# Borders of mixer and post norms joined to their neighbours, attention over two heads at a time

## The reference: what is computed

```python
# first block
h = rmsnorm(x, norm_mix_pre); proj = h @ w_in            # pool, glu, gate_a, gate_b parts
branch_a = pool_mixer(u_pool, ...) ; branch_b = conformer_conv(u_glu, ...)   # conv of 31 taps, layernorm, silu
merged = sigmoid(g_a) * branch_a + sigmoid(g_b) * branch_b
x = x + rmsnorm(merged @ w_o, norm_mix_post)
h = rmsnorm(x, norm_mlp_pre)
x = x + rmsnorm(square(relu(h @ w_up)) @ w_down, norm_mlp_post)
# second block
h = x + deltanet_mixer(rmsnorm_2(x, a_norm), ...)        # 8 heads
h = h + conv_ffn(...)
kv = rmsnorm_2(h, kv_norm) @ kv_w + kv_b                 # 4 key/value heads of 64
h = h + swa_sink_attention(rmsnorm_2(h, b_norm), k, v, w_q, b_q, sinks, w_o, b_o)
h = h + conv_ffn(...)
return rmsnorm_2(h, final_norm)
# attention: 16 heads of 64, blocks of 128 queries that see their own and the previous 128 keys
s = q @ k.T + bias; m = max(max(s), sink); p = exp(s - m)
o = (p @ v) / (sum(p) + exp(sink - m))
```

## Time and profile before

| | |
|---|---|
| three runs | 2055.31, 2057.66, 2059.57 us; median 2057.66 |
| profiled execution | 2061.48 us, span 2059.7 us |
| PE busy | 1969.4 us, 96% of the span |
| DVE, ACT, POOL busy | 1262.3, 765.3, 291.8 us |
| mean granted clock of PE | 0.978 of full speed |
| HBM | 82 GB/s over the span |

### The profile page before, as it was taken

The page is one execution under the profiler, slowest core; times in us unless marked ns, Lnnn a source line. Parts: engine busy times, 40 slices in busy tenths (PEclk is TensorE's granted clock), DMA queues, the critical chain, the costliest instruction groups (busy, mean ns, idle before and its releaser), DMA issues.

```text
span 2059.7 us, 27282 instructions
## 1 busy us (share of the span) xinstructions
PE 1969.4 (96%) x9454; PEld 1631.0 (79%) x9454; DVE 1262.3 (61%) x1826; ACT 765.3 (37%) x1350; POOL 291.8 (14%) x215
## 2 busy tenths in 40 slices
PE   6999889999998899999999999999989999999997
PEld 5878677888887688888887788888778787888886
DVE  5886545333334777777755755737668657657374
ACT  4233344232233433444434433424535434324242
POOL 2433123011112200000012100101100011001011
PEclk9999889999999899999999999999999999999998
DMA  4323231333323011111113232232301132323322
GB/s 172 101 76 90 81 123 62 102 102 92 101 91 105 21 47 51 56 56 46 46 42 94 81 104 90 93 101 92 123 31 42 41 102 82 103 92 92 103 92 82
DMA packets 46922, 170.10 MB, mean 83 GB/s; under 512 B 5344, under 2 KB 5504, under 8 KB 46720
## 3 DMA queue, kind: packets, MB, share of 16 engines
q1 hardware_dynamic: 45648, 165.12, 25.4%
q10 hardware_dynamic: 1200, 3.95, 0.6%
HBM read 166.94 MB, written 2.11 MB: 82 GB/s over the span
## 4 chain that ended last, share of the span: by engine, by line
PE 76%; DVE 7%; issue 2%; ACT 2%; POOL 0%; DVEq 0%; POOLq 0%; ACTq 0%
PE ps L246 16%; PE ps L247 16%; PE ps L248 16%; PE ps L258 6%; PE ps L260 6%; PE ps L259 6%; PE ps L594 2%; PE ps L610 2%; PE ps L1132 1%; PE ps L1157 1%; PE ps L598 1%; DVE scr L1074 1%; PE ps L1143 1%; DVE A_lo L362 1%; DVE X L1932 1%
## 5 line engine op out<-in xcount | busy, mean ns | idle before, releaser
L226 DVE TENSOR_TENSOR w_lo<-w_raw,w_hi 128x1024 fp32r<-128x1024 f32 x293 | 394.9, 1350 | 184.3 <-ACT w_hi L221 184.2
L221 ACT ACTIVATE w_hi<-w_raw 128x1024 fp32r<-128x1024 f32 x304 | 316.9, 1048 | 235.3 <-PE ps L248 169.5
L246 PE MATMUL ps<-A_hi,w_hi 128*128 128x512 f32 x964 | 377.1, 391 | 10.6 <-DVE scr L917 5.0
L247 PE MATMUL ps<-A_lo,w_hi 128*128 128x512 f32 x964 | 376.6, 391 | 0.0
L248 PE MATMUL ps<-A_hi,w_lo 128*128 128x512 f32 x964 | 376.3, 390 | 0.0
L246 PE MATMUL ps<-B_hi,w_hi 128*128 128x512 f32 x732 | 286.8, 392 | 5.4 <-issue 2.4
L247 PE MATMUL ps<-B_lo,w_hi 128*128 128x512 f32 x732 | 285.7, 390 | 0.0
L248 PE MATMUL ps<-B_hi,w_lo 128*128 128x512 f32 x732 | 285.6, 390 | 0.0
L258 PE MATMUL ps<-A_hi,w_hi 128*128 128x512 f32 x460 | 202.0, 439 | 27.5 <-DVE w_lo L226 13.0
L246 PEld LDWEIGHTS ps<-A_hi,w_hi 128*128 128x128 f32 x964 | 181.6, 188 | 50.6 <-issue 12.8
L248 PEld LDWEIGHTS ps<-A_hi,w_lo 128*128 128x128 f32 x964 | 181.9, 189 | 38.1
(11 more groups left out here) (253 smaller groups left out, 2701.0 us busy)
## 6 DMA issues: line engine op xcount, KB each, us to landing
w_raw<-d_ws SPq DMA_DIRECT2D x304, 512.0 KB, 3.5
X<-d_xT SPq DMA_DIRECT2D x4, 512.0 KB, 7.2
X<-d_xT ACTq DMA_DIRECT2D x1, 2048.0 KB, 7.8
d_out<-X SPq DMA_DIRECT2D x4, 512.0 KB, 2.7
scr<-gc_rows ACTq DMA_DIRECT2D x7, 256.0 KB, 3.1
cst<-d_cst SPq DMA_DIRECT2D x1, 800.0 KB, 11.7
par<-d_par SPq DMA_DIRECT2D x1, 344.5 KB, 3.3
scr<-d_pw SPq DMA_DIRECT2D x1, 256.0 KB, 12.4
```

What stands on the lines that cost most here:

```text
L221: nc.scalar.activation(w_hi[:, c], raw[:, c], ACT.Copy).then_inc(S(f"w_hi{s}"), 1)
L226: nc.vector.tensor_tensor(w_lo[:, c], raw[:, c], w_hi[:, c].bitcast(F32), ALU.subtract)\
L246: pe.matmul(ps[bank][:], w_hi[:, c], hi, start=k == 0, stop=False)
L247: pe.matmul(ps[bank][:], w_hi[:, c], lo, start=False, stop=False)
```

## The change

- `spread` uses transposes in place of matmuls with the identity.
- In the first glu round both engines make the splits of the next round's first two units before they evacuate.
- The pool mixer has four buffers UP in place of two, and DVE no longer waits for POOL there.
- At the layer norm `ln_hi` and `ln_lo` of a tile stand one tile later, and the split of branch unit 3 stands before the loop.
- At post0, post1 and fin `sums_early` stands before the last block of the last unit. At post0 the last square is taken from PSUM. Splits on the chain are moved behind it (post0: one, post1: both). In `add_normed` the low part of the previous tile stands before the addition to X.
- Attention: SC and PT have two buffers each, so four with the two heads; scores, transposes and values of both heads of a tile are issued together, scores in two halves of two query blocks, with banks 2 and 3 now belonging to the heads and not to the halves. `part` is cut into 2, 3 and 3 blocks. The query split on ACT and DVE moves by one unit.

```diff
-        UP = [X[...], VATH[:, 0:UPW]]
+        UP = [X[...], VATH[:, 0:UPW], SQ[:, 0:UPW], Y[...]]
...
-                last = pe.matmul(ps[bank][:, c * P:(c + 1) * P], src[:, c:c + 1].broadcast_to([P, P]), ident,
-                                 start=True, stop=True)
+                last = pe.transpose(ps[bank][:, c * P:(c + 1) * P], src[:, c:c + 1].broadcast_to([P, P]), ident)
...
+        def last_unit(pe, r, pair, tag, bank):
+            unit_wait(pe, r, SLOTS - 1)
+            part_blocks(pe, 1, SLOTS - 1, pair, 0, KT - 1)
+            sums_early(pe, tag, KT, bank)
+            part_blocks(pe, 1, SLOTS - 1, pair, KT - 1, KT).then_inc(S(f"unit_done{SLOTS - 1}"), 1)
...
-        def scores_pe(pe, j):
+        def scores_pe(pe, t, n):
+            if n == 0:
+                pe.wait_ge(S("q_t"), count("q_t", t + 1))
+            if t or n:
+                pe.wait_ge(S("s_sc"), count("s_sc", 4 * t + 2 * n))
+            for b in (2 * n, 2 * n + 1):
...
+                for e in range(2):
+                    out = ps[2 + e][:, (b % 2) * 256 + 256 - size:(b % 2) * 256 + 256]
+                    last = pe.matmul(out, half_rows(QT[t % 2], e)[:, b * P:(b + 1) * P],
+                                     half_rows(KA[t % 2], e)[:, lo:lo + size], start=True, stop=True)
...
-            for j in range(2 * KT):
-                t, e = j // 2, j % 2
-                if j < 2 * KT - 1:
-                    scores_pe(pe, j + 1)
-                transpose_pe(pe, j)
-                if e == 0:
-                    part(t + 1, KT // 2, KT)
-                else:
-                    part(t + 2, 0, KT // 2)
-                values_pe(pe, j)
+            scores_pe(pe, 0, 0)
+            part(1, 2, 5)
+            scores_pe(pe, 0, 1)
+            part(1, 5, KT)
+            for t in range(KT):
+                if t < KT - 1:
+                    scores_pe(pe, t + 1, 0)
+                part(t + 2, 0, 2)
+                if t < KT - 1:
+                    scores_pe(pe, t + 1, 1)
+                transpose_pe(pe, t, 0)
+                part(t + 2, 2, 5)
+                transpose_pe(pe, t, 1)
+                part(t + 2, 5, KT)
+                values_pe(pe, t)
...
+            for e in range(2):
+                exps(0, e)
+            ahead(act, split_hi, rnd(U_Q, 0), 0)
+            for t in range(KT):
+                if t < KT - 1:
+                    ahead(act, split_hi, rnd(U_Q, (t + 1) // SLOTS), (t + 1) % SLOTS)
...
+            scored(0, 0)
+            scored(0, 1)
+            maxima(0, 0)
+            maxima(0, 1)
+            ahead(dve, split_lo, rnd(U_Q, 0), 0)
+            q_tile(1)
+            normalise(0, 0)
+            normalise(0, 1)
+            for t in range(KT):
+                more = t < KT - 1
+                if more:
+                    scored(t + 1, 0)
+                    ahead(dve, split_lo, rnd(U_Q, (t + 1) // SLOTS), (t + 1) % SLOTS)
+                    scored(t + 1, 1)
+                    maxima(t + 1, 0)
+                    maxima(t + 1, 1)
+                if t:
+                    output_lo(t - 1)
+                if more:
+                    normalise(t + 1, 0)
+                    if t + 2 < KT:
+                        q_tile(t + 2)
+                    normalise(t + 1, 1)
...
             def glu_round(i, first):
+                if first:
+                    for k in range(2, SLOTS):
+                        ahead(act, split_hi, rnd(U_GLU, i), k)
+                    norm_row(act, "n0")
                 for k in range(SLOTS):
-                    if first and k == 0:
-                        norm_row(act, "n0")
-                    if not first or k > 1:
+                    if not first:
...
+                    if m == KT - 1:
+                        square(act, "post0", m, ps[k % 2][:], 0.5)
                     nc.scalar.activation(tile(Y, m), ps[k % 2][:], ACT.Copy, scale=0.5).then_inc(S(f"evac{k}"), 1)
...
+                    if m:
+                        norm_lo(dve, next_tag, next_g, pairA, m - 1)
                     dve.wait_ge(S(tag + "_t"), count(tag + "_t", m + 1))
                     v.tensor_tensor(tile(X, m), tile(X, m), t, ALU.add).then_inc(S(xtag), 1)
-                    if m:
-                        norm_lo(dve, next_tag, next_g, pairA, m - 1)
...
             token_mean(dve, "post0", 4, D)
-            ahead(dve, split_lo, rnd(U_MLP, 0), 1)
             dve.wait_ge(S("x_back"), count("x_back", 16))
             add_normed("post0", "x1", "mix_post", 5, "n1", "mlp_pre")
+            ahead(dve, split_lo, rnd(U_MLP, 0), 1)
...
-            for k in range(2):
-                ahead(dve, split_lo, rnd(U_DELTA, 0), k)
             add_normed("post1", "x2", "mlp_post", 5, "na", "a_norm")
+            ahead(dve, split_lo, rnd(U_DELTA, 0), 0)
```

More of the change, by code:

```diff
@@ L927, in residual_pe @@
             for i in range(2):
-                for s in range(0 if i else 2, SLOTS):
+                for s in range(0 if i else 2, SLOTS - (closing and i)):
                     unit(pe, rnd(base, i), s, pair, n)
@@ L996, in wait_mid @@
                     pe.wait_ge(S(t + "_lo"), count(t + "_lo", first + k + 1))
-                residual_pe(pe, down, mid, wait_mid, n)
+                last = end and first + n == 22
+                residual_pe(pe, down, mid, wait_mid, n, closing=last)
+                if last:
+                    unit_wait(pe, rnd(down, 1), SLOTS - 1)
+                    part_blocks(pe, 1, SLOTS - 1, mid, 0, n - 1, n)
+                    sums_early(pe, "fin", KT, 4)
+                    part_blocks(pe, 1, SLOTS - 1, mid, n - 1, n, n).then_inc(S(f"unit_done{SLOTS - 1}"), 1)
         def ffn_act(act, L, base, mid, ntag, next_tag, next_g, next_pair, end=False):
@@ L1611, in _, with mlp_group @@
             for i in range(2):
-                for s in range(0 if i else 2, SLOTS):
+                for s in range(0 if i else 2, SLOTS - i):
                     unit(pe, rnd(U_WO, i), s, pairA)
+            last_unit(pe, rnd(U_WO, 1), pairA, "post0", 4)
             norm_pe(pe, "post0", bank=4)
-            def mlp_group(g, first):
+            def mlp_group(g, first, last=False):
                 if first:
@@ L1627, in mlp_group @@
                 for i in range(2):
-                    for s in range(0 if i else 2, SLOTS):
+                    for s in range(0 if i else 2, SLOTS - (last and i)):
                         unit(pe, rnd(U_MLP, g * 4 + 2 + i), s, pairB)
@@ L1701, in _, with ln_hi @@
                 ahead(act, split_hi, rnd(U_BRANCH, 0), k)
+            def ln_hi(j):
+                act.wait_ge(S("ln_z"), count("ln_z", j + 1))
+                nc.scalar.activation(tile(pairB[0], j), tile(CV, j), ACT.Copy).then_inc(S("ln_hi"), 1)
             for j in range(4):
@@ L1710, in _ @@
                     .then_inc(S("ln_th"), 1)
-                act.wait_ge(S("ln_z"), count("ln_z", j + 1))
-                nc.scalar.activation(tile(pairB[0], j), tile(CV, j), ACT.Copy).then_inc(S("ln_hi"), 1)
+                if j:
+                    ln_hi(j - 1)
+            ln_hi(3)
             for k in range(SLOTS):
@@ L1786, in _ @@
             token_mean(dve, "n0", 2, D)
+            for k in range(2, SLOTS):
+                ahead(dve, split_lo, rnd(U_GLU, 0), k)
             def glu_round(i, first):
```

224 lines of the change are left out of this document (109 added, 115 removed).

## The result

The changed kernel takes 2026.07 us (median of four runs, 2025.56 to 2026.37), the kernel before beside it 2058.61 us; the ratio is 0.9844, 95% interval 0.9829 to 0.986. The profiled execution takes 2025.56 us with a span of 2023.8 us, at a mean granted clock of 0.987 in place of 0.978. One execution of all, of the kernel under "A split beside the power", took 3472.6 us at a granted clock of 0.722 and is left out of its median. The forecast was 2026.0 us. The total is right; the parts are not all.

What follows compares the result with a forecast made beforehand. PE, busy 96% of the span, bounds the kernel through work, waits and half clock. Borders 16.4 plus attention 15.4 make 31.8 us off the 2057.7 us median: 2026 us; own range 2018 to 2034, whole range 2016 to 2046.

Steps and rivals of the forecast that it cites:

- Glu border, 5.2 us: Start of the gate units: PE's 3.6 us wait for w_lo and 1.7 us of half clock go, 5.2 us kept.
- Pool buffers, nothing: Pool mixer: four buffers cost and gain nothing, since the wait for POOL isn't in the ring that holds PE.
- Layer norm, 5.7 us: Layer norm border: PE's wait for gated_pool(3) falls from 6.4 to 2.2 us, half clock gains 1.3 us; 5.7 us in all.
- Post norms: Chains at post0, post1, fin: shorter power and spread, less 0.9 us each for sums_early; gains 2.4, 1.1 and 0.15 us.
- I set it at nothing, with 1 us either way: Other order in add_normed: first low part 0.6 us sooner, last about as much later, so no net gain or loss.
- Borders in all: Everything outside attention: 5.2 + 5.7 + 2.4 + 1.1 + 0.15 + 1.8 = 16.4 us gained.
- I take sharing: Middle of attention: both heads' matmuls share the array, a tile falls from 14.1 to 12.1 us; 17.4 us with the ends.
- DVE ... becomes the floor: Middle of attention: DVE, busy 11.3 us a tile, sets the length once PE shares; 0.8 us of handovers make 12.1.
- the ring of DVE, PE and ACT: Rival, attention tile: its ring becomes the bound, 18.1 us without overlap, slower from 16.1 us on; 2071 us, chance 0.05.
- Attention, start, end and clock: Start loses 6.6 us (8.7 us wait for q_tile(1), 1.6 us for two normalises); end gains 1.9, half clock 2.7.
- the borders weren't given back: Rival: glu border's lead ends in the gate stretch, layer norm's drop keeps its length; 5.2 + 3.4 less, 2035 us, chance 0.12.
- no sharing: Rival, attention: the two heads' matmuls don't share the array, 17.4 us of gain fall out; 2043 us, chance 0.25.

Runs made afterwards that it cites:

- A split beside the power: Changed kernel with the low split of the first delta unit again between mean and add_normed at post1: 2028.57 us (median of three).

## Why the prediction was right, and where it was not

**Glu border, 5.2 us:** right; the run that undoes it gives 5.2 by medians.

**Pool buffers, nothing:** right.

**Layer norm, 5.7 us:** right in size; the run that undoes it gives 5.4, of it 5.1 in the stretch. The wait left is 2.8 us, not 2.2 (its own terms, 6.4 less 3.9, give 2.5), and the drop fell to 3.4 us as chosen. In the table the border shows more (5.7 us with 0.9 lost to `sums_early`), since a second drop of 3.4 us, at 252 us before, is gone too.

**Post norms.** The power at 1.02 us and the spread at half are both shown by undoing them. The copy and the split in front of the mean at post0, 1.3 us together, no run undoes. Post0's chain gave 4.0 us, not 3.3; 0.5 of it is the earlier first low part, which the run with the old order in `add_normed` loses again. `sums_early` costs 0.9 us at each border, as forecast, and at post1 0.7 us more: I counted its matmuls, and not that behind the longer wait the last sums mostly run at half clock.

**`add_normed`, "I set it at nothing, with 1 us either way":** wrong, the step of the borders that failed. I counted the tile's instructions by durations from elsewhere and asked which tile's low part came when. What counts is what runs beside them. The new order puts the addition to X beside POOL's squares, and both borders lose 2.9 us. The first low part does come 0.5 to 0.6 us sooner, so the order costs 4.6 us in all where I had nothing. The price stood in the rows that I used: the power that takes 1.93 us beside a split is the same exclusion with the engines' parts changed over, and I applied it to POOL alone.

**Borders in all:** forecast 16.4. The table without attention's 21.6 us (22.1 less a spread's 0.45) sums to 14.3 us; without the 5.7 us of `add_normed` it would be 20. What came on top of the forecast, 3.6 us, is mostly clock. Three stretches gave 1.35, 0.9 and 0.95 us more than forecast, and in each a drop fell away or became 3.4 us shorter: near 252, 710 and 1717 us of the kernel before. The last two places the change doesn't touch. In all, PE's clock was at half for 92 us before and for 55 now. Since executions of one kernel differ in such drops, part of this is chance.

**Attention, middle.** "I take sharing": right. The two heads' matmuls take 3.8 us together in place of 7.0, and with other work between them the whole gain is gone. The rule named there (the Trainium skill, TensorEngine Tiling (Array Packing), section Key Properties) agrees with the trace: 1.75 us for both heads' values in place of 3.5. "DVE ... becomes the floor": right that PE is no longer the bound, since 0.5 us more of its work leaves the length at 11.8. That DVE is the bound is shown in part only. It has 65.1 of 71 us, 10.8 us a tile of 11.8, but the chain that ended last runs in this tile and its neighbours through 5 us of ACT's exponentials and copies as well (tile from 1552.91 us, two pieces of that chain: start, us, what):

```profile
1560.24 1.67 ACT scr L1256 x7
...
1562.95 1.50 ACT scr L1256 x7
```

So it may be the ring of DVE, PE and ACT that the prediction priced as a rival, at 11.8 us and not 16.1; no run takes work from DVE alone or from ACT alone. The forecast of 12.1 took DVE's 11.3 us a tile; it needs 10.8. The tile gives 0.3 us x 7, some 2.2 us, more.

**Attention, start, end and clock.** The wait for `q_tile(1)` was forecast at 8.7 us and is 8.2, and its cause, the exponentials ahead of the split, is shown by moving them. The 1.6 us behind it, for two normalises, didn't come: PE's half-clock scores and two blocks (1516.25 to 1520.4 us) covered them, and its next scores had no wait. The half clock behind it holds 3.7 us of PE's work and not 5, and at the end of attention there is no drop at all. Attention gives 21.6 us, not the 15.4 of the forecast: 2.2 are the tile, 1.6 the normalises and 2.4 the clock.

So the total came out near 31.8 us because 5.7 us lost in `add_normed` met some 6 us more from attention. There is a second piece of luck. For the profiled execution the forecast was 2029.7 us, and it took 2025.56: 35.9 us less, not 31.8. The step to 2026.0 took off another 3.8 us, by which the profiled execution of the kernel before lay above its median. That distance belonged to this one execution, and the changed kernel's is 0.5 us below its median; so taking it off made up for the 4.1 us of gain that the sum lacked by the stages. By medians the gain was 32.5 us. *Rivals:* the borders weren't given back, the tile's ring didn't bind at 16.1 us (a tile has 11.8), and "no sharing" is excluded. That rival priced itself at 17.4 us less gain. The run with other work between the heads lost 31.3, in part by half clock and switches of its own.

## What to carry to other kernels

Before an order of DVE instructions is changed, look at what POOL does at that moment: if DVE's instruction has two inputs in SBUF and POOL's reads SBUF too, they take turns, and an instruction is priced by what it meets. Two matmuls on different halves of the array run together even when they are issued in groups of two to four a head, but not with full-array work between them. Once PE is relieved, what feeds it sets the pace, so read the busy share of the other engines in that stretch first, and the chain that ended last. A wait made a little longer can cost the clock of the short work behind it. And a forecast for the median that starts from one profiled execution inherits that execution's distance from the median.
